# A table of constants is allocated behind all large buffers of a two-block transformer kernel instead of between ring and x

## What is computed

```
# block 1
h = rmsnorm(x, mix_norm_g);  proj = h @ w_in                      # 1024 x 5632
o = three attentions, each @ its w_branch;  merged = sum of gate * o
x = x + merged @ w_out                                            # 1024 x 1024
u = causal_depthwise_conv(rmsnorm(x) @ w_ffn_up)                  # 1024 x 5632
x = x + (silu(u_gate) * u_val) @ w_ffn_down                       # 2816 x 1024
# two layers
x = layernorm(alpha * x + 0.5 * swiglu(x))                        # 1024 x 5632, 2816 x 1024
p = x @ w_mix_in                                                  # 1024 x 11792
merged = gated sum of (diff. attention, ssd, stick-breaking attention) @ w_branch
x = layernorm(alpha * x + merged @ w_mix_out)
x = layernorm(alpha * x + 0.5 * swiglu(x))
```

## Time and profile before

| what | value |
| --- | --- |
| median of 3 runs | 2022.12 us (2021.96 to 2022.37) |
| span of the profiled execution, first to last instruction | 2021.5 us |
| mean granted clock of TensorE | 0.998 of 2.4 GHz |
| PE matmul busy | 2001.2 us, 14178 instructions |
| DVE busy, ACT busy | 1397.6 us, 1097.8 us |
| read from HBM | 351.83 MB, 175 GB/s over the span |

### The profile page before, as it was taken

How to read it: one execution, slowest core, us unless ns; L and a number is a source line. 1 busy time by engine, 2 the same in 40 slices (tenths; PEclk the granted TensorE clock), 3 DMA queues, 4 the chain that set the end, 5 groups by cost and what they waited for, 6 DMA issues and landing times.

```text
span 2021.5 us, 35322 instructions
## 1 busy us (share of the span) xinstructions
PE 2001.2 (99%) x14178; PEld 1827.1 (90%) x14178; DVE 1397.6 (69%) x2098; ACT 1097.8 (54%) x1761; POOL 149.2 (7%) x150
## 2 busy tenths in 40 slices
PE   8999999999999999999999999999999999999998
PEld 7889899899988889998999989998888989899996
DVE  7877688745556686778775656656668677886555
ACT  6686466534444577658544443434558756753442
POOL 1200000000000001710000000000000380000000
PEclk9999999999999999999999999999999999999999
DMA  7534456545745544644645744575454564464563
GB/s 281 167 126 146 157 187 228 188 129 186 254 164 167 167 133 150 199 157 133 221 137 187 249 167 159 186 250 181 142 168 128 166 190 146 147 208 147 187 209 124
DMA packets 272891, 354.71 MB, mean 175 GB/s; under 512 B 10211, under 2 KB 226045, under 8 KB 272765
## 3 DMA queue, kind: packets, MB, share of 16 engines
q1 hardware_dynamic: 271421, 348.71, 52.4%
q0 software_dynamic: 1344, 4.23, 0.8%
HBM read 351.83 MB, written 1.08 MB: 175 GB/s over the span
## 4 chain that ended last, share of the span: by engine, by line
PE 90%; DVE 5%; ACT 3%; issue 1%; POOL 1%; DMA 0%; SPq 0%; DVEq 0%; ACTq 0%
PE ps L808 25%; PE ps L810 17%; PE ps L817 17%; PE ps L818 7%; PE ps L812 7%; PE ps L802 3%; PE ps L804 3%; PE ps L803 3%; DVE ring_r L1963 1%; PE ps L1328 1%; ACT ring_hi L1453 1%; PE ps L1259 1%; PE ps L1051 1%; POOL small L2737 1%; DVE tok_r L1963 1%
## 5 line engine op out<-in xcount | busy, mean ns | idle before, releaser
L1963 DVE TENSOR_TENSOR ring_r<-ring,ring_hi 128x1024 fp32r<-128x1024 f32 x602 | 732.9, 1224 | 412.9 <-ACT ring_hi L1453 410.9
L1453 ACT ACTIVATE ring_hi<-ring 128x1024 fp32r<-128x1024 f32 x602 | 632.4, 1059 | 596.9 <-PE ps L817 372.0
L808 PE MATMUL ps<-xT_hi,ring_hi 128*128 128x256 f32 x2784 | 682.7, 284 | 0.8 <-DVE xT_r L1963 0.8
L810 PE MATMUL ps<-xT_r,ring_hi 128*128 128x256 f32 x2784 | 672.6, 280 | 0.0
L808 PEld LDWEIGHTS ps<-xT_hi,ring_hi 128*128 128x128 f32 x2784 | 525.0, 189 | 16.4 <-issue 11.6
L810 PEld LDWEIGHTS ps<-xT_r,ring_hi 128*128 128x128 f32 x2784 | 525.0, 189 | 0.1
L817 PE MATMUL ps<-xT_hi,ring_r 128*128 128x256 f32 x2784 | 384.4, 280 | 0.0
L817 PEld LDWEIGHTS ps<-xT_hi,ring_r 128*128 128x128 f32 x2784 | 352.4, 188 | 0.0
L2737 POOL TENSOR_TENSOR small<-small,const 128x1 f32<-128x1 f32 (+3 forms) x32 | 39.7, 1242 | 1830.2 <-DVE small L2412 1266.9
L812 PE MATMUL ps<-ring_hi,tok_r 128*128 128x512 f32 x344 | 135.8, 395 | 0.0
L808 PE MATMUL ps<-ring_hi,xT_hi 128*128 128x512 f32 x328 | 132.0, 402 | 1.8 <-DVE xT_r L2106 0.9
(11 more groups left out here) (380 smaller groups left out, 2865.1 us busy)
## 6 DMA issues: line engine op xcount, KB each, us to landing
ring<-in_w_mix_in SPq DMA_DIRECT2D x88, 1024.0 KB, 5.1
ring<-in_ffn_w_in SPq DMA_DIRECT2D x80, 1024.0 KB, 5.1
ring<-in_ffn_w_out SPq DMA_DIRECT2D x44, 1024.0 KB, 4.9
ring<-in_w_branch SPq DMA_DIRECT2D x24, 1024.0 KB, 5.1
ring<-in_w_ffn_up SPq DMA_DIRECT2D x22, 1024.0 KB, 5.1
ring<-in_w_in SPq DMA_DIRECT2D x21, 1024.0 KB, 5.1
ring<-in_w_ffn_down SPq DMA_DIRECT2D x11, 1024.0 KB, 4.9
ring<-in_w_mix_out SPq DMA_DIRECT2D x8, 1024.0 KB, 5.6
```

Of the source, the lines that this page charges most:

```text
L808: pe.matmul(out_, stat[0], mov[0], start=first, stop=False)
L810: pe.matmul(out_, stat[0], mov[1], start=False, stop=False)
L1453: act.activation(half_of(high_of(s), s, q), half_of(ring[:, s % SLOTS, :], s, q), ACT.Copy).then_inc(w_hi, 1)
L1963: return dve.tensor_tensor(lo, whole, hi.bitcast(F32), ALU.subtract)
```

## The change

The line that allocates the table is moved from between `ring_hi` and `x` to the place between `act_j` and `pos`, near the end of the list. The table has 1766 float32, 7,064 bytes per partition. Nothing else changes: the instructions of all engines stand in the same order with the same shapes.

```diff
         ring, ring_lo = both("ring", [P, SLOTS, SLOT])
         ring_hi = sb("ring_hi", [P, HIGHS, SLOT], F32R)
-        const, const_r = both("const", [P, CONST_W])
         x = sb("x", [P, T, D])
...
         stats = sb("stats", [P, T, 12])
         act_j = sb("act_j", [P, P])
+        const, const_r = both("const", [P, CONST_W])
         pos = sb("pos", [P, T], I32)
```

## The result

| | before | after |
| --- | --- | --- |
| median of the timed runs | 2022.02 us (10 runs) | 2027.33 us (10 runs, 2025.83 to 2029.39) |
| ratio, 95% interval | | 1.0029 [1.0021, 1.0037] |
| span of the profiled execution | 2021.5 us | 2026.3 us |
| PE matmul busy | 2001.2 us | 2006.0 us |
| 256-column products with ring held: mean distance of two starts | 117.84 ns | 119.88 ns |

Nine of before's ten executions took 2019.40 to 2023.55 us; the tenth, 2149.71 us, was in a slower state and is left out of the ratio.

The account below looks back on a forecast made before the run. The prediction took the kernel as bound by PE, by the distances between matmul starts. Four terms of zero left the 2021.5 us span, and 0.6 us from span to timed median made 2022.1 us; range 2004 to 2036.

Parts of the forecast that it names:

- What bounds the kernel: Whole kernel: time is the sum of distances between matmul starts on PE, whose matmul row covers 99% of the span.
- Term 1: 9,696 products of 256 columns, streamed operand moving from 32 to 0: zero claimed, with -4 to +4 us allowed.
- Term 2: 2,440 products of 512 columns with ring streaming, held operand moving from 32 to 0: zero claimed.
- Terms 3 and 4: DVE and ACT steps, and transfers including PE's 4.7 us wait for the table: zero each, +-1 us for the wait.
- Twins run slower (256): 256-column loops: operands at one offset lock at 120.0 ns, +20 us alone, 2025 to 2038 with the 512-column gain; chance 0.22.
- no effect: All products: addresses do nothing, or no more than a swap of steady rates; 2022.1 us, range 2018 to 2026; chance 0.45.
- Twins run quicker (512): 512-column products: operands at one offset run at 226.5 ns, -4 to -17 us, 2005 to 2018 us; chance 0.17.
- Alignment really saves: 256-column products: streaming from 0 spares a fetch, up to half of 11 ns each, -53 us, 1969 us; chance 0.11.
- The change does not do what it says: Buffers: ring and ring_hi were aligned already and the table ends at 96; same number as the forecast, no separate chance.
- Flips of steady rate: 256-column loops: a shifted phase can swap the rates 117.3 and 118.7 ns; -4 to +4 us allowed around zero.

Follow-up runs that it names:

- all32: Changed kernel with 32 bytes ahead of ring, so ring, ring_hi and all large buffers start at 32 over a multiple of 128: 2028.98 us, ratio 1.0032.
- micro1: Products alone, without the kernel, 25 pairs of operand starts at 256 and 512 columns: 120.0 and 226.7 ns for equal starts.
- twin_in_place: Kernel before, table left in place, 96 bytes behind it so the operands' starts are alike: 2026.38 us, ratio 1.0029.
- micro3: Products alone, each start difference entered six times behind four matmuls of varying width: at 256 columns, difference 192 gave 113.3 ns three times and 117.8 three times.
- pad160: Changed kernel with 160 bytes ahead of x, restoring the earlier start differences while the table stays at the end: 2021.62 us, ratio 0.9998.
- micro5: Products alone in fp32r with 16 to 128 held columns, four start differences: 113.3 to 117.7 ns at 16 held and 256 streamed columns.
- micro2: Products alone, streamed operand 0 to 240 bytes behind the held one in steps of 16: 113.3 to 120.1 ns at 256 columns, 226.7 to 234.6 at 512.
- pad192: Changed kernel with 192 bytes ahead of x, differences 192 for 256-column and 64 for 512-column products: 1990.52 us, ratio 0.9836.

## Why the prediction was wrong

**What bounds the kernel: right.** It was read as a sum of matmul distances, and the spans of eight kernels follow from two distances and their counts, up to 6 us. (The 0.6 us put around the span in the sum compares a median with another execution's span; each execution took 1.8 us more than its own span, as 2028.11 against 2026.3 us. It moves nothing.)

**Term 1, the step that failed.** "I take zero. My reason is that in the staged rows what differs from the loop is the held operand, at 32 there and at 0 here, and the change doesn't touch the held operand of this class." That looks at each operand by itself. What counts is the relation, and the change made it the one that the staged rows had: alike. The staged chunk was not the nearest row but a measurement of the new state, 120.0 ns in the earlier trace rows. Taken at its value it gives +20 us; the runs gave +19.8. all32, micro1 and twin_in_place show that the relation is the cause: with operands alike at other starts, or with the table in its old place, the distance is 119.9 to 120.0 ns again.

**Term 2, the same step again.** "If it hangs on the streaming one, which stays at 0, the gain is zero, and that I take". The staged 226.5 ns of the earlier trace rows was the value here too; the loop now has 226.7 (227.25 in the mean of all), worth -15.1 us. That the forecast of 2022.1 us came within 5 us is luck: two terms put at zero were +19.8 and -15.1. The six products of 231.7 ns around xbc_r in the earlier trace rows looked like evidence for a graded effect. They were a mixture of pairs alike (xbc_r over wide_r and tok_r) and unlike (ring_r over them), and came to 226.7 when all were alike. The 231 ns of ten staged products in the earlier trace rows was also read wrongly, as "right after an interruption": they follow directly on ring's products of 233 ns (611.12 us), and the stream reaches 226.7 only behind them, which is the memory that micro3 shows.

**Terms 3 and 4: right.** DVE and ACT kept their durations within 2 ns, the table's wait within 0.1 us, and pad160 shows that the table's place is worth nothing (0.9998).

**The rivals.** The one that happened was "Twins run slower (256)", with the 512-column gain of the same rule: 2025 to 2038 us forecast, 2027.33 measured; 836 matmuls per 100 us and 2.72 us for twelve starts, the numbers written down for it, are what the trace shows. It had a chance of 0.22 against 0.45 for no effect. "Twins run quicker (512)" was the other half of the same mechanism, not a rival, and should not have had a chance of its own on the faster side. "Alignment really saves" fell with all32, which has no large buffer aligned and runs as the kernel after. "The change does not do what it says" fell: it does move the operands to multiples of 128 bytes, and ring being there already was no reason for nothing to happen, it was why the pairs became alike.

**The rules weighed there.** The load of 106.7 ns by the Trainium skill (TensorE: Matmul & The Clock Gate, section on LDWEIGHTS) was made a reason for zero in Term 1. micro5 can test the figure, which the trace of before couldn't: the load's row goes from 95 to 189 ns between 16 and 128 held columns, 0.84 ns per column, within 1% of columns over 1.2 GHz, or 107 ns for 128. So the figure holds and the inference from it doesn't: the load's length doesn't set the distance, since an eighth of the held columns leaves 113.3 to 117.7 ns. Of the 16-byte lines of the Trainium skill (SBUF — State Buffer, section on Door 1) the text had already said that they can't explain 226.5 against 233.3. The table of micro2 has whole lines throughout and spreads over 6.8 and 8 ns.

**Flips of steady rate.** I had allowed for two steady rates picked by phase, 4 us either way. They exist (micro3), for before's difference of 160 but not for 0, where all twelve entries tried, six at each width, ended at one rate. So this allowance belonged to the kernel before only.

## What to carry to other kernels

In this kernel a buffer's start mattered in fp32r not for its own alignment but for its distance, modulo 256 bytes, from the other operand of the products in which it takes part: list the pairs, count the products of each class, and choose the padding by a table such as micro2's rather than by roundness, with several entries for each difference, since one stretch can show the better of two rates. And compare two such kernels over several executions: a loop that falls into its other rate was worth 4.7 us here. If some part of a kernel already has the relation that a change will bring everywhere, its distance is the forecast, and an argument about each operand separately is no reason to leave it. When a change moves the time little, look at each class of instruction: here +19.8 and -15.1 us stood behind +5.

## What the runs showed of the hardware

- fp32r products of 128x128 by 256 columns, each with its own load, at 2.4 GHz: 113.3 to 120.1 ns by the difference of the starts in steps of 16 bytes, 123.3 at a difference of 4; 512 columns: 226.7 to 234.6 in the same steps, and 240.0 at 196. In bf16: 109.2 and 215.8 at all twelve differences tried.
- The rule repeats each 256 bytes (256, 512 and 1024 read as 0; 128 doesn't) and needs both starts: four pairs of equal starts gave one number.
- The row of a weight load grows by 0.84 ns per held column in fp32r (95 ns at 16, 189 ns at 128) and lasts 98 ns for 128 columns in bf16; the load's length doesn't set the distance of the products.
- A difference can have several steady rates (113.3 and 117.8 at 192; 117.3 and 118.6 at 160). The products ahead pick one, and it held for over 1,000 products in pad192; 0 (at both widths), 112 (at 256 columns) and 96 (at 512) gave one rate in micro2 and at all six entries of micro3.
- At 384 columns the spread is 173.3 to 176.7 ns, and difference 0 is among the quickest, as at 512; of the three widths tried, equal starts are at a disadvantage at 256 columns alone.
- In a kernel of 2022 us whose PE is busy for 99% of the span, three pads of 448 bytes together gave 1.8% (0.9819 [0.9806, 0.9833]).
